# Two transformer blocks on one core: the opening weights by halves, a post-norm's weight row ahead of its root, and a dense stage's first turn between tiles of products

## The reference

```python
def first_block(x, ...):
    for i in range(2):
        m = hybrid_mixer(x, ...)          # x @ w_in, pooling, chunk attention, stick-breaking attention, @ w_out
        x = layer_norm(ALPHA * x + m, ln1_g[i], ln1_b[i])
        f = swiglu(x, ...) if i % 2 == 0 else moe_swiglu(x, ...)   # 8 experts, top 2
        x = layer_norm(ALPHA * x + f, ln2_g[i], ln2_b[i])
    return x

def rmsnorm(x, g):
    return x * lax.rsqrt(jnp.mean(x * x, axis=-1, keepdims=True) + EPS) * g

def second_block(h, ...):
    for l in range(2):
        y = swiglu_2(rmsnorm(h, ffn1_pre_g[l]), ffn1_w_gu[l], ffn1_w_down[l])
        h = h + 0.5 * rmsnorm(y, ffn1_post_g[l])
        u = rmsnorm(h, mix_pre_g[l])
        ...                               # u @ w_in, three attentions, gates, branches
        h = h + rmsnorm(merged @ w_out[l], mix_post_g[l])
        y = swiglu_2(rmsnorm(h, ffn2_pre_g[l]), ffn2_w_gu[l], ffn2_w_down[l])
        h = h + 0.5 * rmsnorm(y, ffn2_post_g[l])
    return h
```

## Time and profile before

| | |
|---|---|
| time, median of 3 runs | 2807.42 us (2806.43 to 2809.47) |
| the profiled execution's own time | 2806.29 us |
| its span in the profile | 2804.5 us |
| TensorE (matmul) busy | 2580.4 us, 92% |
| VectorE busy | 1799.6 us, 64% |
| ScalarE busy | 1406.1 us, 50% |
| GpSimd busy | 196.9 us, 7% |
| read from HBM | 585.36 MB, 211 GB/s over the span |

### The profile page before, as it was taken

How to read it: one execution, slowest core, us unless ns; L and a number is a source line. 1 busy time by engine, 2 the same in 40 slices (tenths; PEclk the granted TensorE clock), 3 DMA queues, 4 the chain that set the end, 5 groups by cost and what they waited for, 6 DMA issues and landing times.

```text
span 2804.5 us, 32348 instructions
## 1 busy us (share of the span) xinstructions
PE 2580.4 (92%) x11950; PEld 2119.3 (76%) x11950; DVE 1799.6 (64%) x1680; ACT 1406.1 (50%) x1485; POOL 196.9 (7%) x266
## 2 busy tenths in 40 slices
PE   7899998699999999999899897879999989878998
PEld 5678776588888888887687776768878867666786
DVE  4654546588988988888555466755555455665543
ACT  4444344377777776776444344444443444443442
POOL 3000020000000000000320000010014000001100
PEclk9899999699999999999999998989999999989999
DMA  6355452398998998998665333345457533323551
GB/s 240 113 190 193 168 157 91 119 351 343 362 355 340 361 354 340 355 359 314 226 218 186 110 132 128 115 149 210 180 173 248 187 132 139 128 90 136 197 193 60
DMA packets 88119, 592.12 MB, mean 211 GB/s; under 512 B 11288, under 2 KB 11472, under 8 KB 20304
## 3 DMA queue, kind: packets, MB, share of 16 engines
q1 hardware_dynamic: 77456, 558.99, 52.5%
q0 software_dynamic: 10560, 31.74, 4.2%
HBM read 585.36 MB, written 5.32 MB: 211 GB/s over the span
## 4 chain that ended last, share of the span: by engine, by line
PE 80%; DVE 11%; ACT 5%; issue 2%; DMA 1%; POOL 1%; DVEq 0%; ACTq 0%; POOLq 0%
PE pp L568 18%; PE pp L569 18%; PE pp L570 18%; PE acc L568 6%; PE acc L570 6%; PE acc L569 6%; DVE lo_a L1708 3%; ACT hi_a L1236 2%; PE tp L713 2%; PE acc L830 1%; PE tp L580 1%; PE acc L663 1%; PE tp L863 1%; ACT sc L1388 1%; DVE lo_b L1802 1%
## 5 line engine op out<-in xcount | busy, mean ns | idle before, releaser
L568 PE MATMUL pp<-hi_a,uT_hi 128*128 128x512 f32 (+1 forms) x2224 | 898.6, 404 | 48.0 <-DVE uT_lo L1688 22.1
L569 PE MATMUL pp<-lo_a,uT_hi 128*128 128x512 f32 (+1 forms) x2224 | 878.7, 395 | 0.0
L570 PE MATMUL pp<-hi_a,uT_lo 128*128 128x512 f32 (+1 forms) x2224 | 878.5, 395 | 0.0
L1769 DVE TENSOR_TENSOR lo_a<-raw_a,hi_a 128x2048 fp32r<-128x2048 f32 x282 | 651.0, 2310 | 125.2 <-ACT hi_a L1304 125.0
L1304 ACT ACTIVATE hi_a<-raw_a 128x2048 fp32r<-128x2048 f32 x282 | 537.9, 1909 | 4.9 <-DMA raw_a<-in_moe_gu 4.4
L568 PEld LDWEIGHTS pp<-hi_a,uT_hi 128*128 128x128 f32 x2224 | 426.9, 192 | 140.7 <-DVE uT_lo L1688 24.1
L570 PEld LDWEIGHTS pp<-hi_a,uT_lo 128*128 128x128 f32 x2224 | 426.9, 192 | 91.8
L569 PEld LDWEIGHTS pp<-lo_a,uT_hi 128*128 128x128 f32 x2224 | 428.0, 192 | 83.2
L569 PE MATMUL acc<-lo_b,hT_hi 128*128 128x512 f32 x792 | 311.8, 394 | 0.0
L1802 DVE TENSOR_TENSOR lo_b<-raw_b,hi_b 128x2048 fp32r<-128x2048 f32 x116 | 269.2, 2320 | 46.7 <-ACT hi_b L1322 45.3
L1708 DVE TENSOR_TENSOR lo_a<-raw_a,hi_a 128x2048 fp32r<-128x2048 f32 (+1 forms) x92 | 202.4, 2242 | 73.9 <-ACT hi_a L1236 73.3
(11 more groups left out here) (253 smaller groups left out, 2781.1 us busy)
## 6 DMA issues: line engine op xcount, KB each, us to landing
raw_a<-in_moe_gu SPq DMA_DIRECT2D x176, 1024.0 KB, 6.6
raw_b<-in_moe_wd SPq DMA_DIRECT2D x88, 1024.0 KB, 8.4
raw_a<-in_ffn_w_gu SPq DMA_DIRECT2D x88, 1024.0 KB, 6.7
raw_a<-in_w_in SPq DMA_DIRECT2D x72, 1024.0 KB, 6.8
raw_b<-in_ffn_w_down SPq DMA_DIRECT2D x44, 1024.0 KB, 4.9
raw_a<-in_ffn_gu SPq DMA_DIRECT2D x22, 1024.0 KB, 5.9
raw_a<-in_w_out SPq DMA_DIRECT2D x16, 1024.0 KB, 5.9
raw_a<-in_w_branch SPq DMA_DIRECT2D x12, 1024.0 KB, 6.1
```

Source lines behind the costliest of these rows:

```text
L568: nc.tensor.matmul(out_ap, l_hi, r_hi, start=start, stop=False, skip_group_check=True)
L569: nc.tensor.matmul(out_ap, l_hi, r_lo, start=False, stop=False, skip_group_check=True)
L570: return nc.tensor.matmul(out_ap, l_lo, r_hi, start=False, stop=stop, skip_group_check=True)
L1769: ins = nc.vector.tensor_tensor(lo_a[:, slot, cs], raw_a[:, slot, cs], hi_a[:, slot, cs].bitcast(F32), ALU.subtract)
```

## The change

The opening: x comes in two DMAs, one for each tile, with the first half of the first chunk between them (`s_early`) and the second half behind. ScalarE runs a one-column exponential first of all, splits the first half as soon as tile 0 is copied, then the second half, and copies tile 1 behind that. VectorE does its part in the same order. TensorE begins tile 0's first twelve products when the first half is split (`s_earlylo`), waits for the whole chunk ahead of the next twelve, and turns tile 1 between them, as at later stages. The second chunk is split by halves.

The norm: `post_norm` is cut in two. `post_front` waits for the sum of squares (VectorE now counts `s_ss` itself) and multiplies `acc` by the weight row into `merged`. `post_back` waits for the root and makes x = merged x root + x in one operation. `across` and the last norm call one after the other.

The dense stage: with `experts == 1` the head no longer turns chunk 0; gate_up(1) makes tile 0's 24 products, waiting only for tile 0's part of `s_ppv`, then turns chunk 0, and then makes tile 1's products.

```diff
@@ -260,7 +260,9 @@
         s_zero = sem("s_zero")
-        s_xin = sem("s_xin")
+        s_xin = [sem("s_xin0"), sem("s_xin1")]
+        s_early = sem("s_early")
+        s_earlylo = sem("s_earlylo")
         s_al = [sem("s_al0"), sem("s_al1")]
@@ -447,8 +449,12 @@
             n = Tally()
-            sp.dma_start(ident[:, :], a["c_ident"]).then_inc(s_xin, 16)
-            sp.dma_start(x[:, :, :], a["x"][0].rearrange("(t p) d -> p t d", p=P)).then_inc(s_xin, 16)
+            sp.dma_start(ident[:, :], a["c_ident"]).then_inc(s_xin[0], 16)
+            sp.dma_start(x[:, 0, :], a["x"][0, 0:P, :]).then_inc(s_xin[0], 16)
+            sp.dma_start(raw_a[:, 0, 0:2048], a["w_in"][0][:, 0:2048]).then_inc(s_early, 16)
+            sp.dma_start(x[:, 1, :], a["x"][0, P:2 * P, :]).then_inc(s_xin[1], 16)
+            sp.dma_start(raw_a[:, 0, 2048:4096], a["w_in"][0][:, 2048:4096]).then_inc(s_al[0], 16)
+            n["a"] = 1
@@ -526,7 +532,7 @@
             for i in range(N_LAYERS):
-                for j in range(2 if i else 0, D_IN // 512):
+                for j in range(2 if i else 1, D_IN // 512):
                     weight(wide(a["w_in"][i], 512 * j))
@@ -684,15 +690,18 @@
                     pe.wait_ge(s_alo, c.at(a0 + 1))
+                    opening = experts == 1 and isinstance(j, int) and j == 1
                     if c.rest == 0:
...
                     else:
-                        pe.wait_ge(s_ppv, c.half * 4 + (2 * c.rest + ppv0))
+                        pe.wait_ge(s_ppv, c.half * 4 + (2 * c.rest - opening + ppv0))
                     if sparse and isinstance(j, int) and j == 0:
...
                     for tt in range(tiles):
+                        if opening and tt == 1:
+                            turn(Chunk(c.half, c.rest - 1))
                         wait_tile(tt)
@@ -746,7 +755,8 @@
                     gate_up(Chunk(0, 0), Expert(0, 0), 0)
-                    turn(Chunk(0, 0))
+                    if experts > 1:
+                        turn(Chunk(0, 0))
@@ -982,7 +992,7 @@
-            def first_mixer():
+            def first_mixer(i):
@@ -992,8 +1002,13 @@
                         tt, part = n["worked"] // 2 % 2, n["worked"] % 2
-                        if n["worked"] % 4 == 0:
+                        if n["worked"] % 4 == 0 and (i or n["worked"]):
                             slot[0] = take_a()
+                        elif i == 0 and n["worked"] == 0:
+                            pe.wait_ge(s_earlylo, 1)
+                            slot[0] = 0
+                        elif i == 0 and n["worked"] == 1:
+                            take_a()
                         n["worked"] += 1
@@ -1165,11 +1180,11 @@
-            pe.wait_ge(s_xin, 32)
+            pe.wait_ge(s_xin[0], 32)
             pe.sem_inc(s_bused, 2)
             for i in range(N_LAYERS):
-                transpose_rows(x, i == 0)
-                first_mixer()
+                transpose_rows(x)
+                first_mixer(i)
                 transpose_rows(x)
@@ -1190,7 +1205,7 @@
             n = Tally()
-            landed = [0, 0]
+            landed = [-16, 0]
             n["b"], n["bu"] = 1, 2
@@ -1561,12 +1576,18 @@
             act.wait_ge(s_zero, 2)
-            for tt in range(TT):
-                hi_tile(tt)
+            nc.scalar.activation(stat[:, 146:147], zcol, ACT.Exp)
+            hi_tile(0)
+            act.wait_ge(s_early, 16)
+            nc.scalar.activation(hi_a[:, 0, 0:2048], raw_a[:, 0, 0:2048], ACT.Copy).then_inc(s_ahalf, 1)
+            landed[0] += 32
+            n["a"] += 1
+            act.wait_ge(s_al[0], landed[0])
+            nc.scalar.activation(hi_a[:, 0, 2048:4096], raw_a[:, 0, 2048:4096], ACT.Copy).then_inc(s_ahi, 1)
+            hi_tile(1)
             for i in range(N_LAYERS):
                 if i == 0:
-                    hi_chunk_a()
-                    hi_chunk_a()
+                    hi_halves()
                     act.wait_ge(s_rt, 16)
@@ -1888,6 +1909,7 @@
                 n["acc"] += 1
+                n["ss"] += 2 if which is None else 4
                 gained = which is not None
@@ -1907,25 +1929,32 @@
-            def post_norm(tt, slot):
+            def post_front(tt, slot):
+
+                n["ss"] += 1
+                dve.wait_ge(s_ss, n["ss"])
+                link(nc.vector.tensor_tensor(merged[:, tt, :].rearrange("p (h c) -> p h c", h=2),
+                                             acc[:, 2 * tt:2 * tt + 2, :],
+                                             vec[:, slot, :].rearrange("p (h c) -> p h c", h=2), ALU.mult))
+
+            def post_back(tt):
...
                 wait_rstd()
-                o = merged[:, tt, :]
-                link(nc.vector.scalar_tensor_tensor(out=o.rearrange("p (h c) -> p h c", h=2),
-                                                    in0=acc[:, 2 * tt:2 * tt + 2, :], scalar=rstd[:, tt:tt + 1],
-                                                    in1=vec[:, slot, :].rearrange("p (h c) -> p h c", h=2),
-                                                    op0=ALU.mult, op1=ALU.mult))
-                link(nc.vector.tensor_tensor(x[:, tt, :], x[:, tt, :], o, ALU.add))
+                link(nc.vector.scalar_tensor_tensor(out=x[:, tt, :], in0=merged[:, tt, :], scalar=rstd[:, tt:tt + 1],
+                                                    in1=x[:, tt, :], op0=ALU.mult, op1=ALU.add))
                 signal(s_x)
...
                 slot = gain()
-                post_norm(0, slot)
+                post_front(0, slot)
+                post_back(0)
                 signal(s_rows)
...
                 lo_tile(0, True)
-                post_norm(1, slot)
+                post_front(1, slot)
+                post_back(1)
+                n["ss"] += 2
                 signal(s_rows)
@@ -2270,18 +2299,25 @@
             dve.wait_ge(s_zero, 2)
-            dve.wait_ge(s_xin, 32)
-            signal(s_rows)
+            dve.wait_ge(s_xin[0], 32)
             signal(s_rows)
             signal(s_blo)
-            for tt in range(TT):
-                lo_tile(tt)
+            lo_tile(0)
+            n["a"], n["half"] = 1, 1
+            dve.wait_ge(s_ahalf, 1)
+            nc.vector.tensor_tensor(lo_a[:, 0, 0:2048], raw_a[:, 0, 0:2048], hi_a[:, 0, 0:2048].bitcast(F32),
+                                    ALU.subtract).then_inc(s_earlylo, 1)
+            dve.wait_ge(s_xin[1], 16)
+            signal(s_rows)
+            dve.wait_ge(s_ahi, 1)
+            nc.vector.tensor_tensor(lo_a[:, 0, 2048:4096], raw_a[:, 0, 2048:4096], hi_a[:, 0, 2048:4096].bitcast(F32),
+                                    ALU.subtract).then_inc(s_alo, 1)
+            lo_tile(1)
...
                 if i == 0:
-                    lo_chunk_a()
-                    lo_chunk_a()
+                    lo_halves()
                     dve.wait_ge(s_rhi, 1)
@@ -2289,6 +2325,7 @@
                 first_mixer(i)
+                n["ss"] += 6
                 layer_norm(factor=1.0)
@@ -2405,7 +2442,8 @@
             for tt in range(TT):
-                post_norm(tt, slot)
+                post_front(tt, slot)
+                post_back(tt)
```

## The result

| | before | after |
|---|---|---|
| median | 2807.65 us (2804.53 to 2809.47, 6 runs) | 2788.06 us (2785.7 to 2790.22, 6 runs) |
| ratio, 95% interval | | 0.9931 [0.9918, 0.9944] |
| the profiled execution's span | 2804.5 us | 2784.3 us |

The changed kernel is 19.6 us faster. The prediction said 11.9, and its range ended at 2789, so the time lies outside it, on the fast side.

What follows compares the result with a forecast made beforehand. TensorE, busy 92% of the span, was taken as the bound, so only its standing could be won. Gains of 2.7 + 5.5 + 3.7 = 11.9 us gave 2795; own range 2792 to 2798, 8-in-10 range 2789 to 2802.

Steps and rivals of the forecast that it cites:

- Part 1: The opening: first turn of softmax weights 4.4 us earlier, less 1.7 for the clock, so 2.7 us gained.
- the sum's term for the clock: Opening only: after TensorE stands some 3 us, seven products run at the lower clock, costing 1.7 us.
- The mask's transfer: Opening, GpSimd's chain: the third weight chunk overlaps it less, gaining 2.5 us, or nearer 2 by the skill's queue rule.
- the store's issue at 12.91: Opening, GpSimd's chain: the neighbourhood rows' store is issued at 12.91 as before, since nothing ahead of it changes.
- the addition: Opening, first bias: VectorE's split ends before the bias lands, so the 2.92 us addition gets 1.6 us shorter.
- Part 2: The norm behind a stage: acc times weight row overlaps the root, gaining 5.5 us over six norms.
- The root's step: Norm, GpSimd: its first step takes 0.22 us beside VectorE's front operation, which has one operand in PSUM.
- rival C: Norm: the root waits behind the front operation, Part 2 is near 0 and the time 2801; chance 0.07.
- Part 3: The dense stage's first turn: tile 0 of chunk 1 goes first, removing waits ahead of it, 3.7 us gained.
- wait for lo_b: Dense stage, down(0): a wait at the opening down would show rival D; the forecast had 0.4 us to spare.
- rival D: Dense stage: lo_b is 1.1 us late at five stages, time 2801, chance 0.07; with the clock 2814, chance 0.03.

Runs made afterwards that it cites:

- Experiment 5: The changed kernel with the mask's load ahead of the store's waits, and the pool matrix and weights behind the first two heads' biases: 2781.99 us.
- the turn alone: The kernel before with only the dense stage's new order (tile 0's products ahead of chunk 0's turn): 2795.22 us, ratio 0.9954.
- experiment 2: The changed kernel with a memset of 880 columns between post_front and post_back of tile 0 at five norm passages: 2794.35 us.
- experiment 4: Unused products in TensorE's waits at five norm passages: 2 ahead of and 5 behind the turns in before, 2798.26 us; 5 behind in after, 2784.55 us.
- experiment 3: Extra overwritten products in dense stages: before with 3, 6 or 12, 2808.80, 2809.02, 2812.21 us; the turn alone with 18, 2803.97; before padded, 2810.07.
- before padded: The kernel before with 10 extra overwritten products in each of the second block's four dense stages: 2810.07 us, ratio 1.0007.
- before filled: The kernel before with unused products at five norm passages, 2 ahead of the turns of x and 5 behind them: 2798.26 us, ratio 0.9964.

## Why the prediction was wrong

The rows of the waits were read rightly in the main; the step that failed is the clock's. The prediction says that "only time in which TensorE stands still can be won", and parts 2 and 3 put the clock at nothing, as if a wait cost its own length alone; only part 1 charged a longer standstill 1.7 us. Forecast were 13.6 us of waits less 1.7 of clock; measured are 10.2 us less standing, 0.95 behind the last product, and 9.6 to 10.8 gained by the clock (54 fewer slow products), so the sum's term for the clock was wrong by its sign and by 11 to 12 us, and the waits came out 2.5 short. By parts:

- **Part 1, 2.7 us: none measured** (1.0004 alone). Products begin at 12.18 for 11.9. The mask's transfer was 2.5 us shorter, as taken (7.65 for 10.13), and not nearer 2, and the addition 1.65 (1.27 for 2.92). What I had as fixed, the store's issue at 12.91, wasn't: it came at 13.59, since the copy at 10.84 took 1.33 us beside VectorE's first split, while the next one, clear of it, took 0.28. That this could happen was in the rule that the prediction itself cited for part 2 (the Trainium skill, "SBUF — State Buffer", Who interferes with whom: an operation of VectorE with two SBUF inputs contends with GpSimd's reads), and the two rows bear it out. I had applied it to the root, and not to these copies. The store and the bias also took 0.8 us longer (7.72 for 7.53 and 6.63 for 6.03), for which no run shows a cause. So the first turn came 2.68 us earlier, not 4.4, behind 3.91 us of standing, not 3, and by the end of the first mixer 0.5 was left, with 7 more slow products on average, 1.4 us, near the 1.7 that was charged. What ate the rest isn't shown. Experiment 5 shows that the first turn waited for GpSimd's chain: with the mask out of it, 6.1 us.
- **Part 2, 5.5 us: right in the waits.** 0.99 for 0.97, 0.94 for 0.82, and the last norm 0.95 for 0.97 (from 2797.64 to 2801.36 before, from 2778.41 to 2781.18 after). The root's step took 0.22 beside the front operation, so rival C falls. The waits ahead of the turns of x are gone; they were 3.9 us in all, where the sum had 4.55 for these five passages, since two of them had only 0.57 and 0.60 to lose. But behind each stood the wait of 2.34, and the two together drew 8 to 12 slow products (6 to 12 with the turn alone) where in after the one draws 7 or none. Putting 1 us back brought 25 of them back (experiment 2); filling the time took all 56 away, with TensorE's operands ready no sooner (experiment 4). That the standstill draws the slow products is shown. Alone the part gave 13.4.
- **Part 3, 3.7 us: right in the waits.** Two of 1.08 went whole, two fell to 0.57 and 0.56, the first from 1.22 to 0.94: 3.5. No wait for lo_b appeared at the opening down, so rival D falls. What I hadn't looked at is the stage's other end: the same 2.05 us wait is or isn't followed by 7 or 8 slow products, depending on the stage's length (experiment 3). Alone the part took all 29 away and gave 12.5: 11 of the traces' difference are 2.0 us less standing and some 9 of clock, of which these 29 are 5.8; that the other 13 hang on the stages' length isn't shown. In the whole change the passages' slow stretches end at other points, three of the distances are 180.5, 189.9 and 180.8, and 23 came back. That is one reason why the parts don't add up.
- **The range** left this out. The row at hand, a restart at 0.59 worth 1.7 us, was one of some 35 slow stretches in before. Asking of the 56 slow products behind the norms' passages whether they stay would have taken the low end to 2795 - 56 x 0.2 = 2784.

What stays open: why 179.70 to 181.28 us is followed and the strips on either side aren't. The table is a regularity of one kernel's stage, found after the runs; one of its 46 waits broke it, at 181.3 its border is drawn between 181.28 and 181.29, and behind longer distances it says nothing.

## What to carry to other kernels

Price a TensorE wait as its length plus the slow products behind it: here 0.2 us each, up to 12, so that a 0.9 us wait ahead of a 2.3 us one was worth 2 to 3 us. List every restart with a lower granted clock before costing any edit; where the wait can't go, unused products of just its length can fill it, and they must be timed, since too many gave the whole gain back. Where slow products fall can also change with a few tenths of a microsecond of a stage's length, so count more than one trace, and test each part alone and with a pad before crediting its mechanism. And a contention rule that clears one pair of operations must be held against all the others that the change moves together.

## What the runs showed of the hardware

- Equal waits of 2.05 to 2.07 us were followed by 3 us at a granted clock of 0.50 or by none at all; between 178.5 and 182.7 us behind the last slow stretch, the strips of the table, drawn from these waits, told the two apart in 65 of 66.
- Added work of 9.2 us cost 2.2 us in one kernel (before padded), and unused products that made nothing ready sooner gained 10.4 in another (before filled).
- The same code, up to 158 us of the span, had 11 to 23 slow products in nine traces, while the medians of one kernel lay within 0.1% of each other.
- At 12.18 to 17.60 us the granted clock's column shows 1.00 although the products lie 0.43 us apart; at the start of a trace the distance is the better witness.
- A product of 128x256 of plain float32 took two passes, 16 of them 3.27 us or 0.20 each; a 128x512 product of float32r takes one of 0.23.
